# Splitting the first unit of the S5 input projection into a buffer of its own

## What is computed

```
h = rmsnorm(x, ffn_pre_gain[0])
x = x + rmsnorm(swiglu(h, ffn_w_gate[0], ffn_w_up[0], ffn_w_down[0]), ffn_post_gain[0])
h = rmsnorm(x, mix_pre_gain[1])
u = h @ w_in                    # the S5 input projection, 1024 x 1024
...                             # chunked state-space scan over u
```

## Time and profile before

| | us |
|---|---|
| median of 3 runs | 1005.32 |
| lowest and highest | 1005.13, 1005.66 |
| span of the profiled execution | 1002.9 |
| TensorE busy in it | 974.8 |
| DVE, ACT, POOL busy | 616.3, 492.4, 316.2 |

### The profile page before, as it was taken

How to read it: one execution, slowest core, us unless ns; L and a number is a source line. 1 busy time by engine, 2 the same in 40 slices (tenths; PEclk the granted TensorE clock), 3 DMA queues, 4 the chain that set the end, 5 groups by cost and what they waited for, 6 DMA issues and landing times.

```text
span 1002.9 us, 17059 instructions
## 1 busy us (share of the span) xinstructions
PE 974.8 (97%) x6948; PEld 874.4 (87%) x6948; DVE 616.3 (61%) x648; ACT 492.4 (49%) x659; POOL 316.2 (32%) x331
## 2 busy tenths in 40 slices
PE   8999899999999999999999999999989999999997
PEld 6987679999988778788889999887969889999886
DVE  4899766666664555465665555535686665655544
ACT  6765564444433466545564434433566464344332
POOL 5670457799899217761020000001100020000000
PEclk9999999999999999999999999999999999999999
DMA  9742046777666845545555655556963646556551
GB/s 337 267 135 75 1 153 212 229 220 222 221 226 225 251 154 176 168 130 171 159 170 175 198 172 179 199 185 230 389 226 130 204 132 196 179 167 207 170 168 42
DMA packets 131138, 186.79 MB, mean 186 GB/s; under 512 B 4752, under 2 KB 103568, under 8 KB 130576
## 3 DMA queue, kind: packets, MB, share of 16 engines
q1 hardware_dynamic: 106944, 158.28, 48.4%
q10 hardware_dynamic: 24144, 27.81, 8.2%
HBM read 174.54 MB, written 15.73 MB: 190 GB/s over the span
## 4 chain that ended last, share of the span: by engine, by line
PE 86%; DVE 7%; ACT 3%; issue 2%; POOL 2%; ACTq 0%; DVEq 0%; POOLq 0%
PE ps L419 15%; PE ps L421 14%; PE ps L420 14%; PE ps L473 7%; PE ps L477 7%; PE ps L475 7%; PE ps L440 4%; PE ps L442 4%; PE ps L441 4%; DVE cacc L2147 2%; ACT whi L373 1%; PE ps L901 1%; DVE wlo L379 1%; PE ps L920 1%; PE ps L1004 1%
## 5 line engine op out<-in xcount | busy, mean ns | idle before, releaser
L379 DVE TENSOR_TENSOR wlo<-wraw,whi 128x2048 fp32r<-128x2048 f32 x141 | 335.3, 2378 | 229.7 <-ACT whi L373 229.3
L373 ACT ACTIVATE whi<-wraw 128x2048 fp32r<-128x2048 f32 x143 | 273.6, 1914 | 362.2 <-PE ps L421 218.0
L419 PE MATMUL ps<-actH,whi 128*128 128x256 f32 x1232 | 351.7, 285 | 1.4 <-DVE actL L606 1.1
L420 PE MATMUL ps<-actL,whi 128*128 128x256 f32 x1232 | 348.5, 283 | 0.0
L421 PE MATMUL ps<-actH,wlo 128*128 128x256 f32 x1200 | 339.5, 283 | 0.0
L419 PEld LDWEIGHTS ps<-actH,whi 128*128 128x128 f32 x1232 | 236.3, 192 | 5.2 <-issue 3.9
L420 PEld LDWEIGHTS ps<-actL,whi 128*128 128x128 f32 x1232 | 236.4, 192 | 0.1
L421 PEld LDWEIGHTS ps<-actH,wlo 128*128 128x128 f32 x1200 | 230.2, 192 | 0.0
L654 POOL TENSOR_SCALAR ss<-ss 128x1 f32<-128x1 f32 x8 | 2.3, 285 | 455.1 <-ACT sg L627 454.8
L473 PE MATMUL ps<-whi,gH 128*128 128x512 f32 x256 | 79.6, 392 | 0.0
L477 PE MATMUL ps<-whi,gL 128*128 128x512 f32 x256 | 78.9, 389 | 0.0
(11 more groups left out here) (388 smaller groups left out, 1355.8 us busy)
## 6 DMA issues: line engine op xcount, KB each, us to landing
wraw<-in_ffn_w_gate SPq DMA_DIRECT2D x22, 1024.0 KB, 5.5
wraw<-in_ffn_w_up SPq DMA_DIRECT2D x22, 1024.0 KB, 5.5
wraw<-in_ffn_w_down SPq DMA_DIRECT2D x22, 1024.0 KB, 5.0
wraw<-in_fox_w_in SPq DMA_DIRECT2D x16, 1024.0 KB, 5.4
wraw<-in_w_gate SPq DMA_DIRECT2D x11, 1024.0 KB, 5.4
wraw<-in_w_up SPq DMA_DIRECT2D x11, 1024.0 KB, 5.7
wraw<-in_w_down SPq DMA_DIRECT2D x11, 1024.0 KB, 5.1
wraw<-in_w_in SPq DMA_DIRECT2D x9, 1024.0 KB, 11.5
```

The source lines that it names most:

```text
L373: act.activation(self.high_of(n0), self.wraw[:, n0 % RAW, :], ACT.Copy).then_inc(self.hi_done, 1)
L379: dve.tensor_tensor(self.low_of(n0), self.wraw[:, n0 % RAW, :], self.high_of(n0).bitcast(F32), ALU.subtract).then_inc(self.lo_done, 1)
L419: pe.matmul(out, wh, self.actH[:, k, :], start=(i == 0), stop=False)
L420: pe.matmul(out, wh, self.actL[:, k, :], start=False, stop=False)
```

## The change

The first unit of the S5 input joins the list of units apart.

```diff
-        self.apart = (self.first["f2.up"], self.first["f3.up"])
+        self.apart = (self.first["f2.up"], self.first["s"], self.first["f3.up"])
```

## The result

| | us |
|---|---|
| before, median of the 5 runs beside it | 1005.16 |
| changed, median of 5 (lowest, highest) | 1009.82 (1009.08, 1010.61) |
| ratio, with its 95% interval | 1.0043 [1.0031, 1.0055] |
| span of the profiled execution, changed | 1008.1 |

The change makes the kernel slower by 0.43%, 4.7 us. Forecast were +1.5 us, a range up to 1007.9 and "no change" as the likeliest class. The time lies outside the range.

A forecast was written before the change was run, and what follows sets the result against it. TensorE, busy 97% of the span, was taken as the bound. Terms -1.42 - 0.82 + 2.24 + 0.3 + 1.2 gave +1.5 us on the median of 1005.32: 1006.8 us, range 1003.6 to 1007.9.

The forecast's parts named there:

- The early split: End of FFN two: s0's high and low splits run before L488, so L680 and L550 come 1.42 us earlier.
- The clock at L550: End of FFN two: TensorE's stop ahead of L550 shrinks to 0.66 us, keeping full clock and gaining 0.82 us more.
- The later load: glu0's load waits for TensorE to finish s0, lands beside OTab at 724.4; copies of s3 start 0.3 us later.
- The clock at L1655: After s3: TensorE stops 3.2 us ahead of L1655, its clock falls, costing 1.2 us.
- slower outright: Rival at glu0's load: lands 1.7 us behind OTab, at 725.7; +3.3 us, 1008.6, chance 0.13.
- The anchor: Whole kernel: profiled span 1002.9 taken as 2.4 us under the median of 1005.32, to place the forecast time.
- Load late, clock stays: Rival ahead of L1655: glu0 lands late but no second clock fall; +0.3 us, 1005.6, chance 0.30.
- Load in time: Rival at glu0's load: lands by 722, stop stays short, 1.2 to 2.2 us gained; 1003.6, chance 0.17.
- No early split: Rival at FFN two's end: s0's high split held, no gain, later load paid; +3.7, 1009.0, within the 0.13 case.

The follow-up runs named there:

- the warm-up experiment: Kernel before with 30 more small warm-up products at the end of FFN two, ahead of L550: 1005.51 us, ratio 1.0003.
- second profile: Changed kernel run once more, without edits: 1009.03 us.
- the one with warm-up products: Changed kernel with 18 warm-up products of 128x512 between s3 and L1655: 1008.66 us, ratio 1.0028.
- the second pair: Both kernels run once more without edits, for second profiles: kernel before 1006.48 us, changed kernel 1009.03 us.

## Why the prediction was wrong, point by point

- **The early split: right.** 1.42 us at L680 and L550, forecast and measured.
- **The clock at L550: right.** Forecast 0.82; 2.18 in all less 1.42 is 0.76, and the warm-up experiment shows the same 0.76 by itself.
- **The later load: right in mechanism, its landing too early.** Issue forecast 13.9 us after L488, measured 13.91. Landing forecast 30.1 (724.4), measured 31.9, and 31.6 in its second profile and 32.8 in the one with warm-up products. This is the step that failed: I took the *duration* of glu1's transfer, 16.2 us, and added it to the earlier issue. But such a load ends when the other queue is through, and OTab's landing moved by only 0.7 us (from 30.6 to 29.9 after L488), with its duration going from 14.4 to 15.9. It stands behind RTab and the gain vector in ACT's queue, and the gain vector's landing moved by much the same, from 18.3 to 17.5. glu0 came 2.0 us behind OTab's landing in both profiles of the changed kernel and in the one with warm-up products, and 1.8 behind it without the early split; glu1 came 1.7 behind it before. The bound that I had worked out the right way, 1.7 us behind an OTab that lands 0.9 earlier, gave 31.4, half a us from the truth, and I put it at the far end. The copies of s3 started 1.95 us later than before and not 0.3. What I counted as nothing did cost nothing: glu1 held up nothing behind glu0, and though the first half of `T_dram` took 14.3 us to land (10.1 before), it is 7.25 us from L2439 to L1712 in both kernels.
- **The clock at L1655: right in mechanism, too small.** Forecast 1.2 between 0.82 and 1.7, measured 1.66, and 1.48 in the second profile. The lower end came from a place where TensorE in part waited for others; here L1655 and L1664 were TensorE's own work, and I had said that such work pays half of the stretch.
- **The sum** was +1.5. With the two terms as measured it is 1.95 plus 1.66, **+3.6**, as the first pair of profiles shows between L488 and FFN three; in the second pair it is 1.63 plus 1.48, +3.1. The rival *slower outright*, at +3.3, is what happened, and I had given it 0.13.
- **The rest,** some 1.1 us up to the 4.7 of the result, no run ties to the change, and its cause stays open. L488 stands 1.60 us later in the changed kernel's profile than in the first one of before, and 0.55 earlier in the second pair. The 43 later runs of before have medians 0.6 above the 5 runs of the result.
- **The anchor.** I set the profiled span 2.4 us under the median. Device time less span is 1.7 in every run since, so the profiled execution would have taken 1004.6, under the median. That shifts nothing in the sum, which is a difference, but a profile of the favourable end hides what the usual execution pays.
- **Other rivals.** *Load late, clock stays* fell with the windows behind 732. *Load in time* fell, except with OTab out of the way. *No early split* fell with the first rows above. The Trainium skill, "DMA: Bandwidth & Descriptors", section "SWDGE vs HWDGE vs iDMA", has at most 4096 bytes as the preferred size of a packet, beside its description of transfers that GpSimd issues; from it I had estimated a landing of glu0 at 723.4, which is 29.1 us after L488. The traces don't agree: OTab's packets had 32 KB and glu0's 1 KB, and glu0 landed 31.9 us after L488.

## What to carry to other kernels

Freeing a buffer later is a moved transfer, and a moved transfer must be looked at in its new company: here a load in packets of 1 KB barely moved (0.13 MB in 9 us) until the transfer in packets of 32 KB beside it was through. Take the end of such a load from the end of the other queue, and not from a duration. And look at a stop of TensorE twice: once for itself and once for the clock behind it, which here cost 0.76 us behind the stop of 2.08 us and 1.48 to 2.6 us behind those of 3.76 to 4.82 us. Here 8 KB in each partition that were free at that time did the same early split without moving the load, and turned +0.4% into -0.2%.

## What the runs showed of the hardware that I had not expected

- Two queues in one stretch share each DMA engine packet by packet, whatever their sizes: 111 packets of ACT's queue against 128 of SP's with 3.64 and 0.13 MB, and 421 against 418 with 1.54 and 0.43 MB once the large transfer was cut up.
- The same load beside the same transfer took 16.9, 17.7, 17.9 and 18.9 us to land in four profiles.
- In this stage the clock fell for 3.4 us with a stop of TensorE of 2.08, 4.53 and 4.82 us, for 6.8 us with one of 3.76 us, and not with stops of 0.71 to 1.84 us (the last with OTab in parts). The length of one stop does not decide it alone: near 108 us it fell for 6.8 us in the changed kernel behind stops of 0.71 and 1.00 us, and the same two stops left it at 1.00 in the first profile of the kernel before.
- In the dense rows of small products at the end of the scan TensorE paused with nothing awaited that the profile shows ("issue"): for 0.25 to 1.58 us ahead of L1699's products in four of the ten profiles, for 1.37 and 1.44 us in L1712's in two, and not at all in the other four. What brings such a pause and decides its length stays open, and it is as large as the gains of single steps here.
